# Feed-forward weight copies laid out with one, two or four row chunks interleaved, in turn over the units

## The chip, the cores and the metric

The kernel runs on one core of one Trainium2 chip. The metric is device time in microseconds (us); lower is better. The engines that matter here are TensorE (matmuls, PE in the profile, and its loads of the stationary operand, PEld), ScalarE (ACT), VectorE (DVE), GpSimd (POOL) and the queue of SyncE (SP), which issues the weight transfers.

## The reference, cut to what matters

The reference is two transformer-like blocks one after the other. The first has two layers (a Fourier mixer, then differential attention), and after each mixer a SwiGLU feed-forward part; the second is a hybrid of a state-space scan and attention. The change touches only the two feed-forward parts:

```python
def swiglu(h, w_in, w_out):
    gate, up = jnp.split(h @ w_in, 2, axis=-1)
    return (jax.nn.silu(gate) * up) @ w_out

# per layer i: 512 latent rows, and 256 context rows in layer 0 alone
x = x + g2 * swiglu(modulate(rms_norm(x, ...), sh2, sc2), ffn_w_in[i], ffn_w_out[i])
```

`w_in` is 1024 x 5632 and `w_out` 2816 x 1024, float32. The output has to be that of float32 products.

## The kernel before, in words

**Units.** All weights stream through a ring of two slots `ring` in SBUF, each [128, 8, 256] float32: eight row chunks (`kc`, 128 rows of the weight on the partitions) of 256 columns. One such block is a unit, and the plan (`stream_plan`) fixes their order. A feed-forward layer has 22 units `("in", layer, c)` and, after the 8th, the 16th and the 22nd of them, four units `("down", layer, lo, cb)` each. The "down" units of the last group (lo = 16) have six row chunks, all others eight.

**The two copies of a weight block.** A float32 product is made of three products of the rounded type fp32r. ScalarE copies a ring slot to `wH` (the rounded part, `split_hi`, line 1834 for the units here) and VectorE writes the rest, ring minus `wH`, to `wL` (`split_lo`, line 2562). Each of `wH` and `wL` has NS = 2 slots of the same shape [128, 8, 256]. `split_block` gives the three views. A copy is one instruction over the whole block, 2048 elements on each partition (1536 with six chunks). ScalarE starts the copy of a unit when the unit two places before it is done (`unit_end`), since they share the slot.

**The matmuls.** `ffn` takes for each unit `exact`, the list of operands: for each row chunk three pairs (wH with the activations' high part, wH with their low part, wL with their high part), 24 for eight chunks. The first operand, 128 columns of a weight copy, is the stationary one; it is loaded anew for each matmul. `tile` (lines 688 and 693) runs the list for 512 latent columns (line 688) and, in layer 0 alone, runs it once more for 256 context columns (line 693). Each unit has two tiles (`half`, `j`), one for each 128 of its 256 columns. The first "in" unit of each layer, c = 0, has a function of its own (`first_unit`, lines 951 and 953), which reads the copies directly.

**Order around it.** TensorE waits with `weights(key)` for the VectorE copy of a unit (semaphore `w_lo`), and in `begin` for the PSUM banks of the unit two places before. After each "in" unit ScalarE does the SiLU (L1913, L1916), VectorE the product with the up half (L2690, L2693), ScalarE the high copy of the hidden activations (L1920), VectorE their low copy (L2697), and only then come the two copies of the unit two places on. After that, in layer 0, VectorE sums for later conditioning vectors (L2474, L2477), and TensorE turns those into columns (`more_columns`, L744, L755). SyncE refills a ring slot once the VectorE copy out of it is done.

Of the kernel before, what the change touches and what calls it, by code (L numbers as in the profile page):

```python
# [12 lines left out]
P = 128  # L13
D = 1024
KC = D // P
# [16 lines left out]
NS = 2  # L32
# [138 lines left out]
def bass_two_blocks_kernel(nc, io, kt_d, dl_d, dc_d, xsave, out):  # L171
    PLAN = stream_plan()
    N_OF = {key: n for n, key in enumerate(PLAN)}
# [12 lines left out]
    def source(key):  # L186

        kind = key[0]
        if kind == "ada":
            return w_ada[key[1]], 0, KC, 256 * key[2]  # L190
        if kind == "fnet":
            return io["fnet_w_out"][0], 0, KC, 256 * key[1]
        if kind == "down":
            _, layer, lo, cb = key
            return io["ffn_w_out"][layer], P * lo, dict(GROUPS)[lo] - lo, 256 * cb
        if kind in ("dq", "dk", "dv"):
            return io["diff_w_in"][0], 0, KC, {"dq": 0, "dk": D, "dv": 2 * D}[kind] + 256 * key[1]
        if kind in ("xs", "z"):
            return w_in2, 0, KC, {"xs": COL_X, "z": COL_Z}[kind] + 512 * key[1] + 256 * key[2]
        if kind in ("q", "k", "v", "za"):  # L200
            return w_in2, 0, KC, {"q": COL_Q, "k": COL_K, "v": COL_V, "za": COL_ZA}[kind] + 256 * key[1]
        if kind in ("gs", "ga"):
            return w_in2, 0, KC, COL_G + (D if kind == "ga" else 0) + 256 * key[1]
        if kind == "pa":
            return io["w_proj_att_2"][0], 0, KC, 256 * key[1]
        return io["w_out_2"][0], 0, KC, 256 * key[1]

    with ExitStack() as ctx:
# [35 lines left out]
        def apart(name, shape):  # L244

            return sb(name + "H", shape, F32R), sb(name + "L", shape, F32R)
# [13 lines left out]
        wH, wL = apart("w", [P, NS, KC, 256])  # L260
# [254 lines left out]
        def slot_of(n):  # L515

            if n >= EARLY:
                return (n - EARLY) % NR
            if n >= FRONT:
                return (0, 1, NR, NR + 2, NR + 1, NR + 2, NR, NR + 2)[n - FRONT]  # L520
            return n % (NR + 4) if n < 12 else NR + n - 12

        def slot(n):
            i = slot_of(n)
            if i >= NR and n >= FRONT:
                return RS[:].rearrange("p c n -> p (c n)").rearrange("p (i c n) -> p i c n", i=3, n=256)[:, i - NR]
            return ring[:, i] if i < NR else early[:, i - NR]
# [9 lines left out]
        def n_after(key):  # L537

            a, b = N_BEFORE[key]
            return a + (2 if key[0] in ("k", "v", "bc", "xs", "ps") else 1), b + (2 if key[0] in ("k", "bc", "xs", "ps") else 1)  # L540
# [30 lines left out]
        def arrived(n):  # L571

            return sum({"in": 32, "bc": 32, "fnet": 64}.get(PLAN[m][0], 16) for m in range(n + 1) if slot_of(m) == slot_of(n))

        def split_block(n):

            key = SPLIT[n]
            kc = source(key)[2] if key[0] not in ("in", "bc", "ps", "do") else KC
            return slot(N_OF[key])[:, 0:kc], wH[:, n % NS, 0:kc], wL[:, n % NS, 0:kc]


        @block.sync
# [76 lines left out]
        def _(pe):  # L659
            step = [0]  # L660

            def weights(key):

                n = N_OF[key]
                if key[0] != "ada":
                    pe.wait_ge(w_lo, W_OF[key] + 1)
                    return wH[:, S_OF[key] % NS], wL[:, S_OF[key] % NS]
                pe.wait_ge(ring_ready[slot_of(n)], arrived(n))
                return slot(n)

            def begin(key):

                t = step[0]
                assert STEPS[t] == key, (STEPS[t], key)
                step[0] += 1
                if t >= 2:
                    for w in banks_read(t - 2):
                        pe.wait_ge(*w)
                return t % 2
# [17 lines left out]
            def exact(w, a, n, c, wait=None, first=0):  # L697


                parts = []  # L700
                for k in range(n):
                    on = (wait[0], wait[1] + k + 1) if wait else None
                    parts += [(w[0][:, k, c:c + P], a[0][:, k, :], on), (w[0][:, k, c:c + P], a[1][:, k, :], None),
                              (w[1][:, k, c:c + P], a[0][:, k, :], None)]
                return parts

            def ada_rows(i):
# [51 lines left out]
            def more_columns(key):  # L759

                if key not in BESIDE_ADA:
                    return
                j = BESIDE_ADA.index(key)
                if j - 2 in STRIPS and j > 5:
                    strip_cols(j - 2)
                if j - 2 in SUMS:
                    sum_cols(j - 2)
                if j - 1 in STRIPS and j > 4:
                    strip_rows(j - 1)
# [135 lines left out]
            for cb in range(4):  # L905
                begin(("fnet", cb))
                w = weights(("fnet", cb))
                for m in (2 * cb, 2 * cb + 1):
# [4 lines left out]
                    eu, ev, c = bank[2 * (m % 3)], bank[2 * (m % 3) + 1], P * (m % 2)  # L913
                    for k in range(15):
                        p, x, y = k // 3, *((0, 0), (0, 1), (1, 0))[k % 3]
                        wt = w[x][:, p, c:c + P] if p < 4 else w64[x][:, P * m:P * m + P]
                        nc.tensor.matmul(eu[:, 0:UC], wt, uv[y][:, 2 * p, 0:UC], start=k == 0, stop=k == 14)
                    for k in range(12):
                        p, x, y = k // 3, *((0, 0), (0, 1), (1, 0))[k % 3]
# [21 lines left out]
            def first_unit(layer, extra):  # L941

                s = begin(("in", layer, 0))
                w = weights(("in", layer, 0))
                keep_busy(3, 3 * s)
                to = [bank[3 * s], bank[3 * s + 1]]
                more = [bank[3 * s + 2][:, 0:256], bank[3 * (1 - s) + 2][:, 256:512]]

                def product(half, kc, x, y):
                    first, last = kc + x + y == 0, kc == KC - 1 and x == 1  # L950
                    m = nc.tensor.matmul(to[half], w[y][:, kc, P * half:P * half + P], h1[x][:, kc, 0:LAT], start=first, stop=last)
                    if extra:
                        m = nc.tensor.matmul(more[half], w[y][:, kc, P * half:P * half + P], h1[x][:, kc, H1_CTX:H1_CTX + CTX], start=first, stop=last)
                    if last:
                        m.then_inc(tile_done, 1)

                for kc in range(KC + 1):
                    if kc < KC:
                        pe.wait_ge(h_hi, 2 * KC * layer + kc + 1)
                        for half in range(2):  # L960
                            product(half, kc, 0, 0)
                            product(half, kc, 0, 1)
                    if kc:
                        pe.wait_ge(h_ready, KC * (2 * layer + 1) + kc)
                        for half in range(2):
                            product(half, kc - 1, 1, 0)

            def ffn(layer):
                extra = CTX if layer == 0 else 0
                for lo, hi in GROUPS:  # L970
                    for c in range(lo, hi):
                        if c == 0:
                            first_unit(layer, extra)
                            more_columns(("in", layer, c))
                            continue
                        s = begin(("in", layer, c))
                        w = weights(("in", layer, c))
                        for half in range(2):
                            tile(s, half, exact(w, h1, KC, P * half), extra, H1_CTX, (g_full, 1) if extra and c + half == 1 else None)
                        more_columns(("in", layer, c))  # L980
                    for cb in range(4):
                        s = begin(("down", layer, lo, cb))
                        w = weights(("down", layer, lo, cb))
                        for j in range(2):

                            tile(s, j, exact(w, hid, hi - lo, P * j, (g_hid, FC * layer + lo) if cb + j == 0 else None), extra, HID_CTX)
                        more_columns(("down", layer, lo, cb))

            norm_sums(1, True)
            pe.wait_ge(n_rstd, 4)  # L990
            ffn(0)


# [207 lines left out]
            for u in range(4 * HEADS):  # L1201
                f, x = u // 8, u % 8
# [41 lines left out]
            for m in range(8):  # L1244
                if m >= 6:
                    pe.wait_ge(r_res, 32 + m - 5)
                out_part(3, m, bank[m % 6], dD_done)
            norm_sums(3, False)
            ffn(1)


# [6 lines left out]
            for k in range(3 * KC):  # L1258
                kc, a, b = k // 3, *((0, 0), (0, 1), (1, 0))[k % 3]
# [375 lines left out]
            for g, t in scan_times():  # L1635
                key = PERIOD[g][t // 4]
# [10 lines left out]
                if (g, t) == (0, 15):  # L1647
                    a, b = n_after(("bc", 1))
# [34 lines left out]
            a, b = n_after(("gs", 3))  # L1683
# [1728 lines left out]
```

## Time and profile before

| What | us |
|---|---|
| Median of 3 runs | 2473.73 (2472.82 to 2475.1) |
| The profiled execution | 2474.97 |
| Span in its profile | 2472.9 |
| Time of that execution outside the span | 2.1 |
| TensorE matmuls busy | 2402.8 |
| Granted TensorE clock, mean | 0.994 |

The span runs from the first to the last instruction of the program. Busy time of TensorE counts each matmul from its start to its modelled end, and these overlap; so the spacing of the starts of neighbouring matmuls says more about its pace than the durations do. The granted clock is given as a share of 2.4 GHz.

### The profile page before, as it was taken

What the parts mean: (1) busy time and instruction counts of PE and PEld (TensorE: products, weight loads), DVE (VectorE), ACT (ScalarE), POOL (GpSimd) and SP (SyncE); (2) the same over time, 40 slices, a digit from 0 to 9 for tenths busy, and PEclk for the clock granted to TensorE, in tenths of its full rate; (3) what the DMA queues carried; (4) which work ended last, traced back from release to release, by engine and by line L of the source; (5) the groups of instructions that cost most, each with busy time, mean ns of one, the idle gap of its engine ahead of it and who ended that gap; (6) DMA issues with size and microseconds to landing.
All of it is one profiled execution on the core that took longest, in us unless ns stands there. A gap on an engine that the chain in (4) does not pass through costs nothing.

```text
span 2472.9 us, 34710 instructions
## 1 busy us (share of the span) xinstructions
PE 2402.8 (97%) x14354; PEld 2008.6 (81%) x14354; DVE 1297.1 (52%) x2101; ACT 880.1 (36%) x1499; POOL 375.3 (15%) x301
## 2 busy tenths in 40 slices
PE   7999999999999999999999999999999999999999
PEld 6678888888887777656888887988989878877788
DVE  3775625543535776785333336366565445554433
ACT  4332111211224544434222224364545333444422
POOL 0210000000014444501000001143343410000000
PEclk9999999999999999999999999999999999999999
DMA  9734334334321111112333332221222121121222
GB/s 325 202 101 120 120 110 129 120 120 119 107 64 35 52 51 35 35 51 69 97 91 102 98 90 86 69 69 52 69 69 80 58 69 52 52 69 52 80 91 111
DMA packets 252744, 220.79 MB, mean 89 GB/s; under 512 B 7480, under 2 KB 243443, under 8 KB 252204
## 3 DMA queue, kind: packets, MB, share of 16 engines
q1 hardware_dynamic: 249072, 217.92, 29.0%
q8 instruction: 114, 1.87, 0.3%
q10 hardware_dynamic: 3260, 0.58, 0.1%
q14 instruction: 42, 0.34, 0.0%
q0 software_dynamic: 256, 0.07, 0.0%
HBM read 214.26 MB, written 6.29 MB: 89 GB/s over the span
## 4 chain that ended last, share of the span: by engine, by line
PE 59%; ACT 3%; DVE 3%; issue 2%; POOL 1%; DVEq 0%; ACTq 0%; POOLq 0%
PE two L688 10%; PE bank L1357 5%; PE bank L1548 4%; PE bank L688 4%; PE bank L1353 3%; PE bank L1334 3%; PE two L1288 3%; PE bank L1529 2%; PE bank L1054 2%; PE two L1159 2%; PE bank L1185 2%; PE two L1568 2%; PE bank L1024 1%; PE bank L1036 1%; PE two L1300 1%
## 5 line engine op out<-in xcount | busy, mean ns | idle before, releaser
L2573 DVE TENSOR_TENSOR wL<-ring,wH 128x512 fp32r<-128x512 f32 x224 | 181.9, 827 | 225.2 <-ACT wH L1843 225.0
L1834 ACT ACTIVATE wH<-ring 128x2048 fp32r<-128x2048 f32 (+1 forms) x80 | 149.2, 1864 | 270.9 <-PE bank L693 72.9
L2562 DVE TENSOR_TENSOR wL<-ring,wH 128x2048 fp32r<-128x2048 f32 (+1 forms) x80 | 178.9, 2236 | 81.2 <-ACT wH L1834 80.9
L688 PE MATMUL two<-h1H,wH 128*128 128x512 f32 x496 | 195.2, 394 | 0.0
L688 PE MATMUL two<-h1H,wL 128*128 128x512 f32 x496 | 193.4, 390 | 0.0
L688 PE MATMUL two<-h1L,wH 128*128 128x512 f32 x496 | 193.2, 390 | 0.0
L1843 ACT ACTIVATE wH<-ring 128x512 fp32r<-128x512 f32 x224 | 133.6, 623 | 58.5 <-PE bank L1334 21.0
L1913 ACT ACTIVATE gateS<-two 128x512 f32<-128x512 f32 x44 | 26.3, 598 | 330.0 <-PE bank L693 141.8
L2666 DVE SCALAR_TENSOR_TENSOR xT<-two,ada,xT 128x512 f32<-128x512 f32 (+1 forms) x48 | 30.6, 680 | 184.9 <-PE bank L693 65.7
L1357 PE MATMUL bank<-unH,wH 128*128 128x272 f32 (+1 forms) x368 | 112.0, 304 | 3.8 <-ACT cin L2104 2.1
L688 PEld LDWEIGHTS two<-h1H,wH 128*128 128x128 f32 x496 | 93.1, 188 | 20.5 <-issue 1.2
L688 PEld LDWEIGHTS two<-h1H,wL 128*128 128x128 f32 x496 | 93.1, 188 | 19.9
L688 PEld LDWEIGHTS two<-h1L,wH 128*128 128x128 f32 x496 | 93.2, 188 | 18.7
L2477 DVE SCALAR_TENSOR_TENSOR adacc<-ring,cond,adacc 128x256 f32<-128x256 f32 x266 | 106.9, 476 | 0.0
L1357 PE MATMUL bank<-unH,wL 128*128 128x272 f32 (+1 forms) x368 | 105.2, 286 | 0.0
L1357 PE MATMUL bank<-unL,wH 128*128 128x272 f32 (+1 forms) x368 | 105.1, 286 | 0.0
L688 PE MATMUL two<-hidH,wH 128*128 128x512 f32 x264 | 103.8, 393 | 0.0
L688 PE MATMUL two<-hidL,wH 128*128 128x512 f32 x264 | 102.9, 390 | 0.0
L688 PE MATMUL two<-hidH,wL 128*128 128x512 f32 x264 | 102.8, 389 | 0.0
L3209 POOL TENSOR_TENSOR rstd<-rstd,sq 128x768 f32<-128x768 f32 x5 | 11.6, 2330 | 579.8 <-ACT sq L1871 579.5
L2297 ACT ACTIVATE probA<-two,amx 128x144 f32<-128x144 f32 (+3 forms) x64 | 34.6, 541 | 155.9 <-DVE amx L3078 155.8
L1548 PE MATMUL bank<-unH,wH 128*128 128x512 f32 x192 | 88.1, 459 | 0.7 <-ACT vA L2270 0.7
(646 smaller groups left out, 6963.2 us busy)
## 6 DMA issues: line engine op xcount, KB each, us to landing
ring<-in_ffn_w_in SPq DMA_DIRECT2D x88, 512.0 KB, 5.1
ring<-in_w_in SPq DMA_DIRECT2D x40, 1024.0 KB, 5.2
ring<-in_w_ada SPq DMA_DIRECT2D x32, 1024.0 KB, 5.2
ring<-in_ffn_w_out SPq DMA_DIRECT2D x16, 1024.0 KB, 5.2
early<-in_w_ada SPq DMA_DIRECT2D x12, 1024.0 KB, 12.0
ring<-in_diff_w_in SPq DMA_DIRECT2D x12, 1024.0 KB, 5.2
ring<-in_w_proj_ssd SPq DMA_DIRECT2D x8, 1024.0 KB, 5.0
ring<-in_ffn_w_out SPq DMA_DIRECT2D x8, 768.0 KB, 4.6
```

The costliest lines, as they stand in the source:

```text
L688: m = nc.tensor.matmul(bank[3 * s + half], w, r[:, 0:LAT], start=i == 0, stop=i == n - 1)
L1054: m = nc.tensor.matmul(bank[b][:, 256 * (i % 2):256 * (i % 2) + 256], h2[x][:, kc, i * P:(i + 1) * P], w[y][:, kc, :], start=k == 0, stop= ...
L1288: m = nc.tensor.matmul(o[:, at:at + hi - lo], w[y][:, kc, P * j:P * j + P], a[x][:, kc, lo:hi], start=k == 0, stop=k == 3 * KC - 1)
L1334: m = nc.tensor.matmul(bank[b], w[y][:, kc, P * t:P * t + P], ys[x][:, kc, :], start=k == 0, stop=k == 11)
L1353: m = nc.tensor.matmul(bank[b][:, 256 * (t % 2):256 * (t % 2) + 256], un[x][:, kc, META + P * t:META + P * t + P], w[y][:, kc, :], start=k ...
L1357: m = nc.tensor.matmul(bank[b][:, 0:hi - lo], w[y][:, kc, P * j:P * j + P], un[x][:, kc, lo:hi], start=k == 0, stop=k == 3 * KC - 1)
L1548: m = nc.tensor.matmul(bank[6 + j], w[y][:, kc, P * j:P * j + P], un[x][:, kc, META:ALL], start=k == 0, stop=k == 3 * KC - 1)
L1834: nc.scalar.activation(hi, raw, ACT.Copy).then_inc(w_hi, 1)
L1843: nc.scalar.activation(hi[:, 2 * r:2 * r + 2, :], raw[:, 2 * r:2 * r + 2, :], ACT.Copy, scale=colA[:, c:c + 1] if SPLIT[n][0] == "ps" else ...
L2477: m = nc.vector.scalar_tensor_tensor(out=o, in0=w[:, kc, :], scalar=x, in1=o, op0=ALU.mult, op1=ALU.add)
L2562: nc.vector.tensor_tensor(lo, raw, hi.bitcast(F32), ALU.subtract).then_inc(w_lo, 1)
L2573: nc.vector.tensor_tensor(lo, raw, hi.bitcast(F32), ALU.subtract).then_inc(q_lo, 1)
```

## The change

Within a slot of `wH` and `wL`, elements of b neighbouring row chunks are interleaved: column n of chunks b\*a to b\*a + b - 1 stands in b neighbouring words. b is 1 (as before), 2 or 4 by `layout(key)`. The bytes, the operations and their order stay what they are. The high copy writes and the low copy reads and writes this order, and a stationary operand is 128 elements that lie b words, 4, 8 or 16 bytes, apart.

```diff
+        def layout(key):
+
+            if key[0] not in ("in", "down"):
+                return 1
+            turn = (1, 2, 4)[key[-1] % 3]
+            return turn if key[0] == "in" or key[2] < 16 else (1, 2, 2, 1)[key[-1]]
+
+        def chunks(t, key):
+
+            b = layout(key)
+            parts = t.rearrange("p c n -> p (c n)").rearrange("p (a n b) -> p a b n", a=KC // b, b=b)
+            return [parts[:, kc // b, kc % b, :] for kc in range(KC)]
+
+        def laid_out(t, raw, kc, key):
+
+            b = layout(key)
+            if b == 1:
+                return t[:, 0:kc], raw
+            parts = t.rearrange("p c n -> p (c n)").rearrange("p (a n b) -> p a b n", a=KC // b, b=b)
+            return parts[:, 0:kc // b], raw.rearrange("p (a b) n -> p a b n", b=b)
+
         def split_block(n):
 
             key = SPLIT[n]
             kc = source(key)[2] if key[0] not in ("in", "bc", "ps", "do") else KC
-            return slot(N_OF[key])[:, 0:kc], wH[:, n % NS, 0:kc], wL[:, n % NS, 0:kc]
+            raw = slot(N_OF[key])[:, 0:kc]
+            hi, lo = (laid_out(t[:, n % NS], raw, kc, key) for t in (wH, wL))
+            return hi[1], hi[0], lo[0]
...
-                    parts += [(w[0][:, k, c:c + P], a[0][:, k, :], on), (w[0][:, k, c:c + P], a[1][:, k, :], None),
-                              (w[1][:, k, c:c + P], a[0][:, k, :], None)]
+                    parts += [(w[0][k][:, c:c + P], a[0][:, k, :], on), (w[0][k][:, c:c + P], a[1][:, k, :], None),
+                              (w[1][k][:, c:c + P], a[0][:, k, :], None)]
...
-                        w = weights(("in", layer, c))
+                        w = [chunks(x, ("in", layer, c)) for x in weights(("in", layer, c))]
...
-                        w = weights(("down", layer, lo, cb))
+                        w = [chunks(x, ("down", layer, lo, cb)) for x in weights(("down", layer, lo, cb))]
```

By `layout`, in each layer these units have another order than before:

| b (step) | "in" units | "down" units (lo, cb) |
|---|---|---|
| 2 (8 bytes) | c = 1, 4, 7, 10, 13, 16, 19 | (0, 1), (8, 1), (16, 1), (16, 2) |
| 4 (16 bytes) | c = 2, 5, 8, 11, 14, 17, 20 | (0, 2), (8, 2) |

## Rows read from the trace of the kernel before

**Rows 1.** The page, busy time by engine (us, share of the span, instructions).

```profile
PE 2402.8 (97%) x14354; PEld 2008.6 (81%) x14354; DVE 1297.1 (52%) x2101; ACT 880.1 (36%) x1499; POOL 375.3 (15%) x301
```

**Rows 2.** The page, the chain that ended last, its shares by engine.

```profile
PE 59%; ACT 3%; DVE 3%; issue 2%; POOL 1%; DVEq 0%; ACTq 0%; POOLq 0%
```

**Rows 3.** Windows of both feed-forward layers: length, busy PE, PEld, DVE, ACT, POOL, clock.

```profile
155.00:690.00 535.00, 535.00 (x3227) 469.70 (x3226) 262.15 (x495) 100.87 (x112) 0.00 (x0) 1.00 0.37 111
...
1139.00:1500.00 361.00, 360.39 (x1586) 297.32 (x1587) 131.56 (x118) 97.53 (x102) 8.28 (x5) 1.00 0.33 94
```

**Rows 4.** TensorE's groups by form: count, busy us, mean ns; one of three products each.

```profile
L688 PE MATMUL two<-h1H,wH 128*128 128x512 f32 x496 | 195.2, 394 | 0.0
...
L688 PE MATMUL two<-hidH,wH 128*128 128x512 f32 x264 | 103.8, 393 | 0.0
...
L688 PE MATMUL bank<-h1H,wH 128*128 128x512 f32 x176 | 68.5, 389 | 0.0
...
L693 PE MATMUL bank<-h1H,wH 128*128 128x256 f32 x176 | 49.4, 281 | 0.0
...
L693 PE MATMUL two<-h1H,wH 128*128 128x256 f32 x160 | 44.9, 281 | 0.0
...
L688 PE MATMUL bank<-hidH,wH 128*128 128x512 f32 x88 | 34.2, 389 | 0.0
...
L693 PE MATMUL bank<-hidH,wH 128*128 128x256 f32 x88 | 24.7, 281 | 0.0
...
L693 PE MATMUL two<-hidH,wH 128*128 128x256 f32 x88 | 24.7, 281 | 0.0
```

**Rows 5.** The chain in order of time, early in layer 1: start, length, what.

```profile
1156.76 5.44 PE bank L688 x24
1162.20 16.32 PE two L688 x72
1178.52 5.44 PE bank L688 x24
```

**Rows 6.** Timeline of TensorE's matmuls, first and last of ten neighbours: start, length.

```profile
436.81 0.28 PE L693 MATMUL bank<-h1H,wL 128*128 128x256 f32 x1
...
437.89 0.28 PE L693 MATMUL bank<-h1H,wL 128*128 128x256 f32 x1
```

**Rows 7.** Timeline of TensorE's loads, two runs of sixteen before short matmuls.

```profile
1603.15 1.88 PEld L1446 LDWEIGHTS two<-xdt,Mt 128*128 128x128 f32 x16
...
1607.79 1.88 PEld L1407 LDWEIGHTS two<-kt,lseg 128*128 128x128 f32 x16
```

**Rows 8.** Groups of TensorE's loads: count, busy us, mean ns.

```profile
L688 PEld LDWEIGHTS two<-h1H,wH 128*128 128x128 f32 x496 | 93.1, 188 | 20.5 <-issue 1.2 <-DVE xT L2666 0.8
```

**Rows 9.** Line 1782 on ScalarE: minimum, median and maximum in ns.

```profile
L1782 ACT ACTIVATE condz<-colA x2: 202/210/217, 26.1 to 26.2; 128x8 f32<-128x8 f32 x2
L1782 ACT ACTIVATE cond<-colA x2: 193/194/196, 26.3 to 26.4; 128x8 f32<-128x8 f32 x2
```

**Rows 10.** Timeline of ScalarE, VectorE and SyncE in layer 1.

```profile
1173.84 0.63 ACT L1920 ACTIVATE hidH<-gateS 128x512 fp32r<-128x512 f32 x1 [5.56 <-DVE gateS L2690]
1174.38 1.90 ACT L1834 ACTIVATE wH<-ring 128x2048 fp32r<-128x2048 f32 x1
...
1176.31 2.29 DVE L2562 TENSOR_TENSOR wL<-ring,wH 128x2048 fp32r<-128x2048 f32 x1 [1.11 <-ACT wH L1834]
1178.63 1.00 SPq L621 DMA_DIRECT2D ring<-in_ffn_w_in  x2
```

**Rows 11.** VectorE groups by form: count, busy us, mean ns.

```profile
L2697 DVE TENSOR_TENSOR hidL<-gateS,hidH 128x512 fp32r<-128x512 f32 x22 | 15.2, 692 | 15.4 <-ACT hidH L1920 15.4
...
L2998 DVE TENSOR_TENSOR ysL<-bank,ysH 128x512 fp32r<-128x512 f32 x16 | 10.9, 682 | 4.7 <-ACT ysH L2188 4.7
```

**Rows 12.** Timelines in layer 0: a low copy, and the start of a later unit.

```profile
425.35 2.29 DVE L2562 TENSOR_TENSOR wL<-ring,wH 128x2048 fp32r<-128x2048 f32 x1 [0.80 <-ACT wH L1834]
...
438.82 0.47 PE L688 MATMUL two<-h1H,wH 128*128 128x512 f32 x1
```

## The prediction

> **What bounds the kernel now.** I read the page first. TensorE is busy for 97% of the span and is most of the chain that ended last [rows 1, 2]; the other engines are far below it. Then I read windows over the two feed-forward layers, where all edits lie: in both stretches TensorE is busy all the time (535.00 of 535, 360.39 of 361 us) at a granted clock of 1.00, its 2.4 GHz level [rows 3]. Nothing there waits for the copies or for a transfer, so a feed-forward unit costs what TensorE's pace makes of it, and the question is whether the pace changes.
>
> The pace is the spacing of starts. In layer 1 the chain has 24 matmuls of 512 columns in 5.44 us and 72 in 16.32 us, so 0.227 us each [rows 5]. In the context loop of layer 0, ten neighbours of 256 columns start from 436.81 to 437.89 us, nine spacings in 1.08 us, 0.120 us each [rows 6]. Each matmul has a load of 128 stationary columns before it. A load's record lasts 188 ns [rows 8], more than the 0.120 us spacing, so records of loads overlap and are no price. The price is bounded by loads in front of short matmuls: sixteen with 64 moving columns and sixteen with 128 both last 1.88 us in all [rows 7]; without the last record, (1.88 - 0.19)/15 = 0.113 us each. As halving the moving columns changed nothing, that is the load's own pace. So a 512-column matmul leaves its load 0.227 - 0.113 = 0.114 us to spare, a 256-column one 0.007 us. The 256-column loop in layer 0 is where a slower load shows at once.
>
> **The change part by part.**
>
> *Counts.* An eight-chunk unit has 2 tiles x 24 = 48 matmuls on line 688 in each layer and 48 more on line 693 in layer 0. Check: line 688 has 3 x (496 + 176 + 264 + 88) = 3072 in both layers, line 693 3 x (176 + 160 + 88 + 88) = 1536, which is half, as it should be [rows 4]. Units with step 16: 7 "in" and 2 "down" in each layer, 9 x 48 = 432 matmuls a layer on line 688 (864 in all) and 432 on line 693. Units with step 8: 7 "in", 2 "down" of eight chunks and 2 of six (36 each), 9 x 48 + 72 = 504 a layer on line 688 (1008) and 504 on line 693. Nothing is added or removed in instructions, bytes, waits or transfers, and no step is moved.
>
> *Stationary loads.* The trace of before has no load with a step above one element, so the price is bounded from both sides. Below: 0, a load goes by its 128 columns at 0.113 us whatever their step. A gain is excluded as far as the rows reach: the 256-column loop runs at 0.120 us against a load pace of 0.113, so at most 0.007 x 432 = 3 us could come even if the loads cost nothing, and nothing here makes them cheaper. Above: I take the nearest row in which only the step differs, ScalarE's line 1782. Eight elements written 128 bytes apart (condz) took 202 to 217 ns, eight written 8 bytes apart (cond) 193 to 196 [rows 9]: 15.5 ns more by the means, 1.9 ns an element. On 128 elements that would be 0.25 us, a load of 0.36 us. It is another engine, a write, and two records on either side, so it is only an end. What speaks for nothing: TensorE reads a moving operand of 512 columns in at most 0.227 us [rows 5], 2.3 elements a ns, and a load asks for 128 in 0.113 us, 1.1 elements a ns. A read path that fell to half its pace at step 16 would still nearly feed a load. I take 0, with the doubling right behind it.
>
> *What a slower load would cost.* A matmul's spacing is then the longer of its own and its load's. Load doubled at step 16, 0.226 us: 432 x (0.226 - 0.120) = 45.8 us on line 693; on line 688 0.226 is still under 0.227, so 864 x 0 = 0. If the load also adds the 0.013 us or so by which the two just touch, 864 x 0.013 = 11 us more. Load at 1.5 times, 0.170: 432 x 0.050 = 22 us. Load at three times, 0.339: 432 x 0.219 + 864 x 0.112 = 191 us.
>
> The Trainium skill (Advanced Engine Details and Errata, "SBUF Cachelines") speaks against this change: SBUF has lines of 16 bytes, and an access pattern wants at least two hits in each for full pace. By it steps of 4 and 8 bytes cost nothing and a step of 16 does; it gives no amount, and no row of before shows it for a load. GPSIMD Engine Reference ("Performance pitfalls for Q7 kernels") has about 2.9 instead of 1.9 cycles an element for GpSimd's reads with steps above 8 bytes; carried over to the load, an estimate, the sum would be that of the 1.5 times above.
>
> *Copies.* ScalarE's copy takes 1.90 us and VectorE's 2.29 us for 2048 elements [rows 10]. With b = 2 or 4 the pattern has one dimension more; VectorE rows of 512 elements in one piece and in four pieces of 128 took 692 and 682 ns [rows 11], so the dimension costs nothing. The step may cost: 0 below, above 1.9 ns an element as in rows 9, which is 3.9 us on either copy. Both lie beside TensorE's work. In layer 1 a unit of 48 x 0.227 = 10.88 us ended at 1162.20 + 10.88 = 1173.08 us [rows 5]; the copies that followed ended at 1178.60 [rows 10], and TensorE needed them at 1183.96, a cover of 5.36 us. In layer 0 the cover is 438.82 - 427.64 = 11.2 us [rows 12]. If both copies doubled, 1.9 + 2.3 = 4.2 us more, still under 5.36: cost 0. At the upper end 7.8 us would be 2.4 late in each of 9 units of layer 1: 22 us. Behind a late copy VectorE's next SiLU product and SP's refill of the ring [rows 10] would also come later, both with most of a unit to spare. I take 0.
>
> *Sum.* 0 on top of the profiled execution's 2474.97 us (span 2472.9 and 2.1 around it), which is 1.2 above the median. Against the median of 2473.73 I predict 2474.
>
> **The rivals.**
>
> *A. No effect* (forecast): the load keeps its 0.113 us at every step, the copies are covered. 2474, own range 2471 to 2478. For it: the load asks for half of what the moving side gets. Against it: only 0.007 us of room on line 693.
>
> *B. The load doubles at 16 bytes, not at 8.* It decides from the point where a load passes 0.120 us. 45.8 us: 2520 (2515 to 2531 with the doubts above). For it: the 1.9 ns of rows 9 shows that some engine pays for a wide step. Against: no read of rows 9 is strided. The cacheline rule of the Trainium skill named above would give this side.
>
> *C. The load takes three times or more at 16 bytes.* Then line 688 pays too: +191 us, 2665 and above. For it: rows 9 carried over whole. Against: that is one write of eight elements.
>
> *D. 8 bytes costs as 16 does*, doubled: (432 + 504) x 0.106 = 99 us, 2573. For it: nothing but the absence of a row.
>
> *E. Copies alone become late* in layer 1, by more than 5.36 us together: up to +22, 2496. For it: rows 9 is ScalarE, the engine that writes the copy; against: both would have to more than double.
>
> *F. A load of 1.5 times*, 2496, line 693 alone.
>
> **How the numbers follow.** A 0.45, B 0.33, C 0.07, D 0.06, E 0.04, F 0.03, and 0.02 for something faster that no row shows. A is the likeliest by itself, so the time is 2474. 8 in 10 takes A, B, E and F: 2471 to 2528; C and D and the top of B are left out. Within 0.2% (5 us, about what a measurement of this kernel can tell from no change) is A, 0.45; slower is B to F, 0.53; faster 0.02.
>
> **What would show it.** Under A the spacing on line 693 is 0.120 us and on line 688 0.227 in all units, in turn over c; line 1834 and line 2562 may have a second, longer duration for every third unit without TensorE waiting. Under B line 693 has 24 matmuls in about 5.4 us instead of 2.9 for c = 2, 5, 8 and so on, and layer 1 is unchanged. Under C layer 1's units of step 16 last over 10.88 us as well, at b = 4 only; under D those of step 8 show it. Under E gaps stand on TensorE ahead of the b = 4 units of layer 1, released by VectorE's line for the low copy. The prediction is wrong if a load at 16 bytes passes 0.125 us, since 432 x 0.012 is already 5 us.

## The result, and the profile after

The changed kernel takes 2538.71 us (median of 4 runs, 2535.43 to 2539.95) against 2473.28 for the kernel before: a ratio of 1.0267, interval 1.0251 to 1.0282, so 65 us slower. The profiled execution is 2538.51 us with a span of 2536.4. I had forecast 2474 with a range to 2528; the time lies 11 us above the range, on the side of rival B.

The page after: TensorE by engine, then the groups of both copies (line, engine, out<-in, count | busy us, mean ns | idle before). The edit moved the lines by 23: 711 and 716 are the latent and the context loop, 1857 and 2585 the copies.

```profile
PE 2464.9 (97%) x14354; PEld 2104.5 (83%) x14354; DVE 1326.8 (52%) x2101; ACT 919.0 (36%) x1499; POOL 375.1 (15%) x301
...
L1857 ACT ACTIVATE wH<-ring 128x2048 fp32r<-128x2048 f32 (+1 forms) x80 | 188.7, 2358 | 272.3 <-PE two L716 79.4
L2585 DVE TENSOR_TENSOR wL<-ring,wH 128x2048 fp32r<-128x2048 f32 (+1 forms) x80 | 208.2, 2602 | 119.1 <-ACT wH L1857 118.9
```

Counts are those of before [rows 1]; TensorE is as full as before, so the 63.5 us of span went into its pace. Its pace in the context loop of the unit c = 5 (step 16), ten neighbours of the timeline, first and last (start, length):

```profile
267.19 0.40 PE L716 MATMUL bank<-h1H,wH 128*128 128x256 f32 x1
...
269.29 0.40 PE L716 MATMUL bank<-h1H,wH 128*128 128x256 f32 x1
```

Nine spacings in 2.10 us are 0.233 us each, where [rows 6] had 0.120. The load before each has a record of 0.33 us (188 ns in [rows 8]), and loads start as often, 0.23 us apart:

```profile
267.06 0.33 PEld L716 LDWEIGHTS bank<-h1H,wH 128*128 128x128 f32 x1
267.29 0.33 PEld L716 LDWEIGHTS bank<-h1L,wH 128*128 128x128 f32 x1
```

In layer 1, the chain in order of time for c = 1 (step 8) and the later tile of c = 3 (step 4) [rows 5 has 5.44 for all]:

```profile
1208.21 5.60 PE two L711 x24
1213.81 5.60 PE bank L711 x24
1219.41 16.74 PE two L711 x72
1236.15 5.44 PE bank L711 x24
```

5.60/24 = 0.233 us with step 8, 5.44/24 = 0.227 with step 4; the 72 are both tiles of c = 2 (step 16) and the first of c = 3, (16.74 - 5.44)/48 = 0.235 us. The copies around it, timeline of ScalarE and VectorE, of a step of 16 and one of 4 bytes:

```profile
1242.89 3.92 ACT L1857 ACTIVATE wH<-ring 128x2048 fp32r<-128x2048 f32 x1
...
1254.10 1.90 ACT L1857 ACTIVATE wH<-ring 128x2048 fp32r<-128x2048 f32 x1
...
1246.84 3.90 DVE L2585 TENSOR_TENSOR wL<-ring,wH 128x2048 fp32r<-128x2048 f32 x1 [3.13 <-ACT wH L1857]
...
1256.03 2.29 DVE L2585 TENSOR_TENSOR wL<-ring,wH 128x2048 fp32r<-128x2048 f32 x1 [1.11 <-ACT wH L1857]
```

Both copies are 2.0 and 1.6 us longer at step 16 and, for c = 5, end at 1250.74 us, before TensorE asks for them at about 1252.8 (the unit of c = 3 ends at 1236.15 + 5.44, that of c = 4 two tiles of 5.60 later).

For the account I took the mean spacing of each tile, from the start of its first matmul to that of its last (23 or 17 spacings), in every unit and both traces; the difference, times the number of matmuls:

| Loop | step 8: spacing, us | step 16: spacing, us | total us |
|---|---|---|---|
| context, layer 0 (before 0.118 to 0.120) | 0.121 | 0.228 | 0.9 + 47.3 |
| latent, layer 0 (before 0.227 to 0.234) | 0.233 to 0.238 | 0.240 to 0.245 | 2.6 + 5.0 |
| latent, layer 1 (before 0.227) | 0.233 | 0.235 | 3.4 + 3.6 |
| units of step 4, all loops | | | under 0.1 |

The sum is 62.7 of 63.5 us. (The terms are rounded. The 0.228 is a tile's mean; its first spacing is still 0.12, the other 22 are 0.233.) In layer 0 the latent loop looks dearer at step 16 than in layer 1, but only by how a tile begins: its first spacing grew by about 0.12 us (0.31 to 0.44 in the first tile of c = 5), and the other 22 are 0.235 as in layer 1. One more difference is on the chain: the copy ahead of layer 1's first units took 2.06 instead of 1.90 us.

### The profile page after: what moved, and what is told of

It reads as the page before. It is cut to its first block, busy times and chain, and to the rows that moved or that the text cites. A ratio compares the mean times of both kernels' runs of the same rounds, so it can differ in the third digit from the quotient of the medians.

```text
span 2536.4 us, 34710 instructions
## 1 busy us (share of the span) xinstructions
PE 2464.9 (97%) x14354; PEld 2104.5 (83%) x14354; DVE 1326.8 (52%) x2101; ACT 919.0 (36%) x1499; POOL 375.1 (15%) x301
## 3 DMA queue, kind: packets, MB, share of 16 engines
q8 instruction: 114, 1.87, 0.3%
## 4 chain that ended last, share of the span: by engine, by line
PE 58%; DVE 3%; ACT 3%; issue 2%; POOL 1%; DVEq 0%; ACTq 0%; POOLq 0%
PE two L711 10%; PE bank L1380 4%; PE bank L1571 4%; PE bank L711 4%; PE bank L1376 3%; PE bank L1357 3%; PE two L1311 3%; PE bank L1552 2%; PE bank L1077 2%; PE two L1182 2%; PE bank L1208 2%; PE two L1591 2%; PE bank L1047 1%; PE bank L1059 1%; PE two L1323 1%
## 5 line engine op out<-in xcount | busy, mean ns | idle before, releaser
L1857 ACT ACTIVATE wH<-ring 128x2048 fp32r<-128x2048 f32 (+1 forms) x80 | 188.7, 2358 | 272.3 <-PE two L716 79.4
L2585 DVE TENSOR_TENSOR wL<-ring,wH 128x2048 fp32r<-128x2048 f32 (+1 forms) x80 | 208.2, 2602 | 119.1 <-ACT wH L1857 118.9
L711 PEld LDWEIGHTS two<-h1H,wH 128*128 128x128 f32 x496 | 115.6, 233 | 14.1 <-issue 1.2
L711 PEld LDWEIGHTS two<-h1H,wL 128*128 128x128 f32 x496 | 115.5, 233 | 12.8
L711 PEld LDWEIGHTS two<-h1L,wH 128*128 128x128 f32 x496 | 115.7, 233 | 11.9
```

Source lines behind the costliest of these rows:

```text
L711: m = nc.tensor.matmul(bank[3 * s + half], w, r[:, 0:LAT], start=i == 0, stop=i == n - 1)
L1857: nc.scalar.activation(hi, raw, ACT.Copy).then_inc(w_hi, 1)
L2585: nc.vector.tensor_tensor(lo, raw, hi.bitcast(F32), ALU.subtract).then_inc(w_lo, 1)
```

## Experiments

**Loads or copies.** Each of the two kernels keeps one half of the edit.

```diff
 # loads_only: old copies, strided stationary operands
-            hi, lo = (laid_out(t[:, n % NS], raw, kc, key) for t in (wH, wL))
-            return hi[1], hi[0], lo[0]
+            return raw, wH[:, n % NS, 0:kc], wL[:, n % NS, 0:kc]
 # copies_only: interleaved copies, neighbouring words loaded
-            return [parts[:, kc // b, kc % b, :] for kc in range(KC)]
+            return [t[:, kc, :] for kc in range(KC)]
```

Expected of loads_only:

> This kernel keeps the strided stationary operands but writes the copies in the old order, so that the loads read mixed words and the output isn't the reference's. Theory L (the loads alone cost): the spacings of the matmuls on the latent and the context loop, summed over the units of the changed kernel, are 62.7 us over those of before, and they come back whole: 2473.3 + 62.7 = 2536 us, context loop at 0.228 us in every third unit, ScalarE's copies all at 1.90 us. Theory C (the slow copies disturb TensorE, by shared access to SBUF): the context loop stays near 0.120 us and the time near 2475 to 2490 us.

Expected of copies_only:

> This kernel writes the copies in the interleaved order but loads 128 neighbouring words, so that the stationary operands mix chunks and the output isn't the reference's. Theory L: the copies take 3.92 and 3.90 us in every third unit, as in the changed kernel, beside TensorE's work, and the time is that of before within 2 us, 2472 to 2476 us; only the copy ahead of the first units of layer 1 is on the chain, at 0.15 us. Theory C: a large part of the 65 us is here, 2490 us or more, with slower spacings while the copies run.

Measured: loads_only 2538.75 us, ratio 1.0261 (1.0247 to 1.0276), the whole loss. copies_only 2473.95 us, ratio 0.9999 (0.9989 to 1.0009), although its copies are as slow as in the changed kernel. Groups by form, first of copies_only, then of loads_only (count | busy us, mean ns):

```profile
L2585 DVE TENSOR_TENSOR wL<-ring,wH 128x2048 fp32r<-128x2048 f32 x72 | 194.8, 2705 | 115.6 <-ACT wH L1857 115.6
...
L1857 ACT ACTIVATE wH<-ring 128x2048 fp32r<-128x2048 f32 x72 | 175.5, 2438 | 229.2 <-PE two L716 58.5 <-PE bank L716 57.3 <-PE bank L1311 34.8
...
L716 PE MATMUL bank<-h1H,wH 128*128 128x256 f32 x176 | 49.4, 281 | 0.0
```

```profile
L2584 DVE TENSOR_TENSOR wL<-ring,wH 128x2048 fp32r<-128x2048 f32 x72 | 166.5, 2313 | 78.8 <-ACT wH L1856 78.8
...
L1856 ACT ACTIVATE wH<-ring 128x2048 fp32r<-128x2048 f32 x72 | 137.2, 1906 | 256.5 <-PE two L715 70.8 <-PE bank L715 64.2 <-PE bank L710 36.6
...
L715 PE MATMUL bank<-h1H,wH 128*128 128x256 f32 x176 | 54.4, 309 | 0.0
```

In copies_only the copies are long (2438 and 2705 ns on average) and the context matmuls those of before (281 ns, [rows 4]); in loads_only it is the other way round. Theory C, that the slow copies disturb TensorE, falls. The cost is the strided load alone, and the copies' 3.6 us are covered as the prediction had it.

**One step at a time.**

```diff
-            turn = (1, 2, 4)[key[-1] % 3]
+            turn = (1, 2, 1)[key[-1] % 3]      # step8_only
+            turn = (1, 1, 4)[key[-1] % 3]      # step16_only, and (1, 1, 1, 1) for lo = 16
```

Expected of step8_only:

> Turn 1, 2, 1: only the units of step 8 bytes are left. By the spacings of the changed kernel they cost 0.9 us in the context loop, 2.6 in layer 0's latent loop and 3.3 in layer 1: 6.8 us, 2480 us. The rival (two words in each 16-byte line are enough for full pace) says 0: 2473.3 us within 1. If the loss at step 8 in the changed kernel came from its neighbours of step 16, this also gives 0.

Expected of step16_only:

> Turn 1, 1, 4: only the units of step 16 bytes are left. By the spacings of the changed kernel: 47.3 us in the context loop, 5.0 in layer 0's latent loop, 3.6 in layer 1: 55.9 us, 2529 us. With step8_only it should sum to the changed kernel's 65 us within 2; if not, the two steps act on each other through the ring or the copies.

Measured: step8_only 2480.60 us, ratio 1.0030 (1.0021 to 1.0039), 7.5 us; by its spacings 6.8. step16_only 2528.10 us, ratio 1.0220 (1.0206 to 1.0235), 55 us; by its spacings 55.8. Together 62.5 of 65 us, 3 us short where I had expected 2; the intervals of the two ratios are wider than that, and by the spacings it is 62.6 of 62.7: the steps are independent. Step 8 isn't free: its interval lies above 1.002.

**One loop at a time.** Old copies; the strided view goes to one loop, the neighbouring words to the other.

```diff
-            return [parts[:, kc // b, kc % b, :] for kc in range(KC)]
+            return [(parts[:, kc // b, kc % b, :], t[:, kc, :]) for kc in range(KC)]
...
+                    x, y = ((v[k][0][:, c:c + P], v[k][1][:, c:c + P]) for v in w)
+                    parts += [(x, a[0][:, k, :], on), (x, a[1][:, k, :], None), (y, a[0][:, k, :], None)]
 # latent_only: the latent loop takes w[0], the context loop w[1]; context_only: exchanged
```

Expected of latent_only:

> Copies in the old order; only the 512-column latent loop loads with the steps 1, 2, 4 in turn (mixed words, so the output isn't the reference's), the context loop loads neighbours. By the spacings of the changed kernel: 2.6 + 5.0 us in layer 0 and 3.3 + 3.6 in layer 1, 14.5 us, 2488 us. A rival says that the latent loop is slowed only by what the context loop leaves behind it: then layer 0 shows 0 and the whole 7 us, 2480.

Expected of context_only:

> The other half: only the 256-column context loop of layer 0 loads with the steps (mixed words again). 47.3 us at 16 bytes and 0.9 at 8 bytes: 48.2 us, 2521 us, spacings of 0.228 and 0.121 us; layer 1 as before. With latent_only it sums to 62.7 us if the two loops don't act on each other.

Measured: context_only 2521.39 us against 2474.76, ratio 1.0192 (1.0177 to 1.0207), 47 us, 47.5 by its spacings. latent_only 2485.53 us, ratio 1.0052 (1.0035 to 1.0069), 11 to 13 us, 13.0 by its spacings; the latent loop of layer 0 lost its 7.6 us with plain loads in the context loop, so the rival falls. The two sum to 60.5 by the spacings, 2.2 us under the changed kernel. Of that, 1.8 us is the context loop of latent_only, which ran a little faster in the strided units than before (0.1185 instead of 0.120 us, 0.1135 instead of 0.118 in "down"); I can't explain it.

**The price of a load by its step.** Old copies, seven steps in turn over c.

```diff
+            s = (1, 2, 3, 4, 6, 8, 15)[key[-1] % 7] if key[0] == "in" else 1
+            flat = t.rearrange("p c n -> p (c n)")
...
+                return flat[:, start:start + n * s].rearrange("p (n b) -> p b n", b=s)[:, 0, :]
```

> Copies in the old order; the loads of the in units c with c % 7 = 0 to 6 step by 4, 8, 12, 16, 24, 32 and 60 bytes (words of other chunks, the output isn't the reference's). Theory R (an engine gets a 16-byte line of SBUF each 1.78 ns, so a load of 128 columns takes 128 x min(step, 16)/16 x 1.78 ns, and never less than its 0.113 us): context spacings 0.120, 0.121, 0.171, 0.228, 0.228, 0.228, 0.228 us. Rival H (full pace below 16 bytes, half from there): 12 bytes stays at 0.120. Rival B (banks or distance): it goes on rising at 24, 32 or 60 bytes.

Measured in a single run, 2568.11 us. Tile means in us, the same within 0.003 in a second unit of each step where there was one:

| step, bytes | 4 | 8 | 12 | 16 | 24 | 32 | 60 |
|---|---|---|---|---|---|---|---|
| context loop | 0.120 | 0.121 | 0.171 | 0.228 | 0.223 | 0.237 | 0.225 |
| latent loop, layer 1 | 0.227 | 0.233 | 0.235 | 0.235 | 0.238 | 0.244 | 0.239 |

The timeline of the 12-byte unit, first and last of 18 neighbours:

```profile
209.46 0.34 PE L723 MATMUL two<-h1H,wH 128*128 128x256 f32 x1
...
212.41 0.34 PE L723 MATMUL two<-h1H,wL 128*128 128x256 f32 x1
```

2.95/17 = 0.174 us: 1.36 ns a column, three quarters of the 0.233/128 = 1.82 ns at 16 bytes, as three quarters of a new line a column would make it. For the load theory R stands; its rivals H (12 bytes free) and B (rising with the distance, not the prediction's B) fall, and 24 to 60 bytes differ from 16 by some per cent.

The latent row follows no such price. The first tile of the 12-byte unit c = 2 in layer 1, first and last of its 24 matmuls:

```profile
1248.15 0.40 PE L718 MATMUL two<-h1H,wH 128*128 128x512 f32 x1
...
1253.56 0.39 PE L718 MATMUL two<-h1H,wL 128*128 128x512 f32 x1
```

5.41/23 = 0.235 us, as much as at 16 bytes, although this load takes 0.174 us and the matmul beside it 0.227. So the latent loop's loss isn't that the load outlasts the matmul.

**The same on the copies.** Interleaving 1, 2, 4 or 8 chunks by c % 4, and 3 in two "down" units; loads of neighbouring words.

```diff
-            turn = (1, 2, 4)[key[-1] % 3]
-            return turn if key[0] == "in" or key[2] < 16 else (1, 2, 2, 1)[key[-1]]
+            turn = (1, 2, 4, 8)[key[-1] % 4]
+            return turn if key[0] == "in" or key[2] < 16 else (1, 3, 3, 1)[key[-1]]
```

> Loads of neighbouring words (mixed chunks, the output isn't the reference's); the copies interleave 1, 2, 4 or 8 chunks by c % 4 (4, 8, 16, 32 bytes), and 3 (12 bytes) in the down units (16, 1) and (16, 2) with 1536 elements. Theory R, with the price of a line from the two engines' 16-byte copies (1.8 ns an element): ScalarE 1.90, 2.04, 3.92, 3.92 us for 2048 elements and, at 0.75 x 1.8 = 1.35 ns, 1536 x 1.35 + 0.2 = 2.3 us for 12 bytes (1.47 before); VectorE 2.29, 2.29, 3.90, 3.90 and 2.2 (1.76 before). Rival H: 12 bytes as before, 1.47 and 1.76. Time as before within 3 us, since all is covered but the copies at the entry of layer 1.

Measured in a single run, 2473.51 us against 2473.50. Timeline of ScalarE and VectorE at 8, 16 and 32 bytes, then at 4 and 12 bytes with 1536 elements:

```profile
1183.47 2.05 ACT L1856 ACTIVATE wH<-ring 128x2048 fp32r<-128x2048 f32 x1
...
1194.35 3.83 ACT L1856 ACTIVATE wH<-ring 128x2048 fp32r<-128x2048 f32 x1
...
1205.23 4.11 ACT L1856 ACTIVATE wH<-ring 128x2048 fp32r<-128x2048 f32 x1
...
1455.47 1.47 ACT L1856 ACTIVATE wH<-ring 128x1536 fp32r<-128x1536 f32 x1
...
1466.35 2.25 ACT L1856 ACTIVATE wH<-ring 128x1536 fp32r<-128x1536 f32 x1
...
1185.55 2.29 DVE L2584 TENSOR_TENSOR wL<-ring,wH 128x2048 fp32r<-128x2048 f32 x1 [1.26 <-ACT wH L1856]
...
1198.21 3.88 DVE L2584 TENSOR_TENSOR wL<-ring,wH 128x2048 fp32r<-128x2048 f32 x1 [3.04 <-ACT wH L1856]
...
1209.38 4.21 DVE L2584 TENSOR_TENSOR wL<-ring,wH 128x2048 fp32r<-128x2048 f32 x1 [3.32 <-ACT wH L1856]
...
1468.63 2.25 DVE L2584 TENSOR_TENSOR wL<-ring,wH 128x1536 fp32r<-128x1536 f32 x1 [1.46 <-ACT wH L1856]
```

12 bytes took 2.25 us on both, expected 2.3 and 2.2. ScalarE's 8 bytes took 2.05 instead of 1.90, VectorE's the same 2.29. Half a line an element, 0.91 ns, is under the pace of both (0.93 and 1.12 ns), so theory R doesn't explain ScalarE's 0.15 us. 32 bytes took 7 to 9% longer than 16.

**The moving operand.** The kernel before, with the context loop reading latent columns at a step.

```diff
+            def stepped(r, b):
+                if b == 1:
+                    return r[:, 0:256]
+                return r[:, 0:LAT].rearrange("p (n b) -> p b n", b=b)[:, 0:b // 2, :]
...
-                                             r[:, at:at + extra], start=i == 0, stop=i == n - 1)
+                                             stepped(r, t_now[0]), start=i == 0, stop=i == n - 1)
...
+                        t_now[0] = (1, 2, 4)[c % 3]
```

Expected of moving_step:

> The kernel before with one edit: the moving operand of the context loop is 256 of the latent columns, at step 4, 8 and 16 bytes in turn over c (4 in the down units), so the context rows of the output are wrong. Theory R: 256 columns at 8 bytes need 128 lines, 0.228 us, at 16 bytes 256 lines, 0.456 us; 336 x 0.108 + 336 x 0.336 = 149 us more, 2622 us. Rival H (two words in a line are enough): 8 bytes stays at 0.120, 16 bytes goes to 0.24, 40 us more, 2514 us. Rival S (only the stationary side is slow): 0.

Expected of moving_ladder, which has steps of 4, 8, 12, 16, 32 and 64 bytes:

> As moving_step (moving operand of the context loop from the latent columns, the context rows of the output are wrong), with steps 4, 8, 12, 16, 32, 64 bytes by c % 6. moving_step gave 0.120, 0.229 and 0.233 us at 4, 8 and 16 bytes, so theory R with lines of 16 bytes at 1.78 ns is wrong for the moving side. Theory M (the moving side fetches 8 bytes in 0.9 ns, so a step of 8 bytes or more costs the same): 0.120, 0.229, 0.229 to 0.233, 0.233, 0.233, 0.233 us. Rival B (distance counts): it rises at 32 and 64 bytes.

Measured: moving_step 2551.55 us, moving_ladder 2567.49 us, a single run each. Timeline of moving_step, first and last of nine at 8 bytes, and of nine at 16 bytes:

```profile
253.11 0.41 PE L701 MATMUL two<-h1L,wH 128*128 128x256 f32 x1
...
254.95 0.41 PE L701 MATMUL two<-h1H,wH 128*128 128x256 f32 x1
...
276.09 0.41 PE L701 MATMUL bank<-h1L,wH 128*128 128x256 f32 x1
...
277.96 0.41 PE L701 MATMUL bank<-h1H,wH 128*128 128x256 f32 x1
```

1.84/8 = 0.230 and 1.87/8 = 0.234 us. All three theories of the first run fail: 8 bytes costs what R said, but 16 bytes doesn't double again; H is right at 16 bytes alone, and S, which had 0, at neither. The ladder's tile means are 0.120, 0.229, 0.228, 0.233, 0.217 and 0.219 us: the moving side doubles at once at 8 bytes and stays, as theory M had it (0.9 ns a column).

**One load in three.** Only the loads of wL are strided.

```diff
-            return [parts[:, kc // b, kc % b, :] for kc in range(KC)]
+            return [parts[:, kc // b, kc % b, :] if low else t[:, kc, :] for kc in range(KC)]
```

> Copies in the old order, and only the loads of wL, one in three, have the steps 1, 2, 4 (mixed words, the output isn't the reference's). If each strided load pays for itself: context loop at 16 bytes (0.228 + 2 x 0.120)/3 = 0.156 us on average, latent loops a third of their loss, in all 62.7/3 = 21 us, 2495 us. If the latent loop's loss of 0.007 to 0.012 us is a state of a whole run of loads (not of each load), it vanishes here or stays whole: 16 or 31 us.

Measured: 2496.80 us against 2473.50, ratio 1.0099 (1.0081 to 1.0117), 23 us, 22.6 by its spacings. In the context loop each strided load pays for itself, timeline at 16 bytes:

```profile
262.08 0.40 PE L715 MATMUL bank<-h1H,wL 128*128 128x256 f32 x1
262.31 0.28 PE L715 MATMUL bank<-h1H,wH 128*128 128x256 f32 x1
262.43 0.28 PE L715 MATMUL bank<-h1L,wH 128*128 128x256 f32 x1
262.55 0.39 PE L715 MATMUL bank<-h1H,wL 128*128 128x256 f32 x1
```

0.23, 0.12, 0.12 us. The latent loop is neither: in layer 1 a third of the loads strided leaves 5.9 of the 8.3 ns at 16 bytes and 4.3 of the 6.7 at 8 bytes. (Layer 0, with its slow tile starts, keeps 1.8 of 5.0 us and 1.6 of 2.6.) Layer 1 shows neither a third nor the whole, so what a strided load does there isn't a price of its own length.

## Why the prediction was wrong, point by point

- **What bounds the kernel, and where a slower load shows.** Right: the loss is TensorE's pace, 62.7 of 63.5 us, and 47.3 of it at step 16 in the 256-column loop with its 0.007 us of room. Counts 432 and 504 were right.
- **The step that failed: "I take 0" for the stationary load at 16 bytes.** It measured 0.233 us, over twice the 0.113 of [rows 7]. The reason I gave was that a load asks for 1.1 elements a ns where the moving side gets 2.3, so half the pace would still nearly feed it. The error was to treat both as one path. Measured one by one, a load gets 128/0.233 = 0.55 elements a ns at 16 bytes and the moving side 256/0.234 = 1.1: each side has its own price for a step. The nearest row, [rows 9], pointed to a price and I used it as an end only; its 1.9 ns an element (15 ns over eight elements, not the 15.5 that I wrote) is what ScalarE's and VectorE's copies (3.9 us for 2048) and the load (1.82 ns a column) turned out to pay, as the whole price of an element and not, as I used it, on top of the old one.
- **"On line 688 0.226 is still under 0.227: 0."** This part of the sum, 0 as well, measured 14.5 us: 8.6 at 16 bytes, near my doubt of 0.013 x 864 = 11 us, and 5.9 at 8 bytes, which nothing in the sum allowed for. The rule behind it, that a spacing is the longer of the matmul's and the load's, failed on this loop. At 16 bytes the load's 0.233 us is over the 0.227, which would look like the cause; but at 12 bytes a load of 0.174 us cost the same, and at 8 bytes one of at most 0.121 us made it 0.233. For the 256-column loop the rule held.
- **Step 8 in the context loop,** which the forecast and B had at 0. Nearly right, 0.9 us.
- **The copies.** Right: at 16 bytes the two took 3.6 us more together, below the 4.2 us of both doubling, and the cover of 5.36 us held: cost 0, shown by copies_only. My upper end, 3.9 us more on either, counted an added 1.9 ns where 1.9 is the whole price.
- **The rivals.** B was the mechanism: its 45.8 us measured 47.3 on the loop it named. Its sign that layer 1 stays unchanged was wrong (7 us there). Its upper end of 2531 left out step 8, 6.8 us; with it, it would have been 2538. C, D, E and F didn't occur. The range should have gone past B's top, since the doubts on line 688 belonged to the case that held a third of the chance.
- **The Trainium skill** (Advanced Engine Details and Errata, "SBUF Cachelines"), whose two hits in each 16-byte line would give B's side: the loads and the copies agree, 8 bytes almost free, 16 bytes at twice the time (1.7 times on VectorE). Beyond it, 12 bytes already costs three quarters of the full price in the load (1.36 ns against 1.82), so for them the time follows the lines fetched for each element, not a bound at two hits. The moving operand disagrees: at 8 bytes it still has two words in each line and took 0.230 instead of 0.120 us.

Shown: the loss is the strided load; in the 256-column loop, where three quarters of it lie, its price up to a step of 16 bytes is that of 16-byte lines at 1.8 ns each, and the copies pay the same price unseen. Open: why a 512-column matmul loses 0.007 us beside a load at 8 bytes and 0.009 beside one at 12, whose own times (at most 0.121 and 0.174 us) are far below 0.227, why one strided load in three costs it more than a third, and why the plain context loop of latent_only ran faster than before. That load and moving reads share something is a guess that these runs neither show nor exclude.

## What to carry to other kernels

Before a stationary operand is given a step, compare the spacing of its matmuls with 128 x (bytes of the step, up to 16)/16 x 1.8 ns: here a float32 step of 16 bytes hid almost wholly behind 512 moving columns and doubled the time of 256. A load that fits still isn't free: at 8 and 12 bytes it cost the 512-column matmuls 0.007 and 0.009 us each. Copies on ScalarE and VectorE follow the same count, and theirs cost nothing as long as the cover is longer. A bound taken from the moving operand's path didn't hold for the load; where the nearest row shows a price, put the likeliest value near it.

## What the runs showed of the hardware that I had not expected

- ScalarE writing at 16 bytes, VectorE reading and writing at 16 bytes, and TensorE loading at 16 bytes all come to 1.8 to 1.9 ns an element (3.92 and 3.90 us for 2048, 0.233 us for 128). VectorE's reading and writing weren't taken apart.
- A moving operand of 256 float32 columns takes 0.230 us at a step of 8 bytes and no more at 12 to 64 bytes (0.217 to 0.233).
- Steps beyond 16 bytes aren't quite alike: loads 0.223, 0.237 and 0.225 us at 24, 32 and 60 bytes, copies 3.8 to 3.9 and 4.1 to 4.2 us at 16 and 32.
- A strided load slows 512-column matmuls that leave it time to spare: 0.227 to 0.233 us beside a load of at most 0.121 us (8 bytes), to 0.235 beside one of 0.174 us (12 bytes).
